# Attention loop of a decoder layer: exponentials first on ScalarE, and weight transposes and values one step earlier

## The reference

```python
xn = rms_norm(h, norm1_g)
proj = xn @ w_in                      # split into gq gk gv gr glr dq dk dv
o_gla  = gla_mixer(gq, gk, gv, gr, glr, ...)       # gated linear attention, 4 heads
o_diff = diff_attention(dq, dk, dv, ...)           # 4 heads, two score maps each
h = h + concat([o_gla, o_diff]) @ w_out
h = h + hier_moe(rms_norm(h, norm2_g), ...)        # 32 experts, top-2 of one group

# diff_attention, for each block of 128 queries
logits = q @ k.T + bias[rel_bucket(qpos - kpos)]   # causal; for comp 0 and comp 1
p = softmax(logits)
w = p[comp 0] - lam * p[comp 1]
out = rms_norm(w @ v, subln_g) * (1 - lambda_init)
```

## Time and profile before

| | us |
|---|---|
| median of 3 runs | 1276.71 (1272.01 to 1277.06) |
| the profiled execution | 1274.93 |
| its span, first to last instruction | 1273.2 |
| PE busy | 1161.4 (91%) |
| DVE busy | 873.3 (69%) |
| ACT busy | 686.3 (54%) |
| POOL busy | 229.5 (18%) |

### The profile page before, as it was taken

How to read it: one execution, slowest core, us unless ns; L and a number is a source line. 1 busy time by engine, 2 the same in 40 slices (tenths; PEclk the granted TensorE clock), 3 DMA queues, 4 the chain that set the end, 5 groups by cost and what they waited for, 6 DMA issues and landing times. The chain is left out here.

```text
span 1273.2 us, 16875 instructions
## 1 busy us (share of the span) xinstructions
PE 1161.4 (91%) x5886; PEld 874.4 (69%) x5887; DVE 873.3 (69%) x1195; ACT 686.3 (54%) x875; POOL 229.5 (18%) x265
## 2 busy tenths in 40 slices
PE   6989998889998779999539999999999999999994
PEld 5868886657665468888436777777777777777772
DVE  4434224655565566665359999999999999999882
ACT  5424204444444343432127777777777777777772
POOL 2212103221111011011022112211221222122100
PEclk9999999999999789999758999999999999999997
DMA  8120210200200244332588999999999999999941
GB/s 306 42 92 1 99 67 1 75 25 30 87 25 17 96 127 152 124 113 83 210 300 297 371 366 372 391 380 371 381 387 373 371 387 385 374 370 386 382 145 25
DMA packets 66271, 273.31 MB, mean 215 GB/s; under 512 B 12004, under 2 KB 18728, under 8 KB 41512
## 3 DMA queue, kind: packets, MB, share of 16 engines
q1 hardware_dynamic: 55592, 245.32, 50.3%
q0 software_dynamic: 7168, 20.98, 7.2%
q10 hardware_dynamic: 3456, 6.29, 1.3%
HBM read 248.44 MB, written 28.32 MB: 217 GB/s over the span
## 5 line engine op out<-in xcount | busy, mean ns | idle before, releaser
L1790 DVE TENSOR_TENSOR experts_w_low<-w_raw,experts_w_high 128x2048 fp32r<-128x2048 f32 x192 | 439.0, 2287 | 60.1 <-ACT experts_w_high L1786 60.0
L1786 ACT CAST experts_w_high<-w_raw 128x2048 fp32r<-128x2048 f32 x192 | 366.0, 1908 | 89.9 <-PE experts_py L1804 52.6
L1802 PE MATMUL experts_ph<-experts_w_high,experts_xT_high 128*96 128x512 f32 x512 | 205.1, 401 | 4.8 <-DVE experts_w_low L1790 3.6
L1803 PE MATMUL experts_ph<-experts_w_low,experts_xT_high 128*96 128x512 f32 x512 | 203.5, 397 | 0.0
L1804 PE MATMUL experts_ph<-experts_w_high,experts_xT_low 128*96 128x512 f32 x512 | 202.2, 395 | 0.0
L1718 POOL DMA_INDIRECT experts_xg<-xn_dram,experts_token x32 | 75.6, 2362 | 384.4 <-DVE experts_token L1698 384.1
L1802 PEld LDWEIGHTS experts_ph<-experts_w_high,experts_xT_high 128*96 128x96 f32 x512 | 84.7, 165 | 39.8 <-DVE experts_w_low L1790 3.7
L1804 PEld LDWEIGHTS experts_ph<-experts_w_high,experts_xT_low 128*96 128x96 f32 x512 | 83.3, 163 | 36.7
L1803 PEld LDWEIGHTS experts_ph<-experts_w_low,experts_xT_high 128*96 128x96 f32 x512 | 83.4, 163 | 33.3 <-issue 0.3
L1802 PE MATMUL experts_py<-experts_w_high,experts_hT_high 128*96 128x512 f32 x256 | 103.0, 402 | 1.2 <-DVE experts_hT_low L1921 1.2
L1803 PE MATMUL experts_py<-experts_w_low,experts_hT_high 128*96 128x512 f32 x256 | 101.8, 398 | 0.0
(11 more groups left out here) (276 smaller groups left out, 2029.3 us busy)
## 6 DMA issues: line engine op xcount, KB each, us to landing
w_raw<-in_moe_w SPq DMA_DIRECT2D x192, 1024.0 KB, 10.9
slot_raw<-in_w_in SPq DMA_DIRECT2D x12, 1024.0 KB, 7.3
front_x<-in_x SPq DMA_DIRECT2D x8, 512.0 KB, 10.9
slot_raw<-in_w_out SPq DMA_DIRECT2D x4, 1024.0 KB, 6.2
front_hx<-in_x SPq DMA_DIRECT2D x8, 512.0 KB, 4.1
out<-front_hx SPq DMA_DIRECT2D x8, 512.0 KB, 2.7
xn_dram<-front_xn SPq DMA_DIRECT2D x8, 512.0 KB, 2.8
gr_dram<-front_stage ACTq DMA_DIRECT2D x8, 256.0 KB, 2.0
```

The costliest lines, as they stand in the source:

```text
L1786: nc.scalar.copy(wh[slot(c, e)][:], raw[:, u, c, :]).then_inc(w_high, 1)
L1790: nc.vector.tensor_tensor(wl[slot(c, e)][:], raw[:, u, c, :], wh[slot(c, e)][:].bitcast(F32), ALU.subtract).then_inc(w_low, 1)
L1802: nc.tensor.matmul(out, x_hi, w_hi, start=start, stop=False)
L1803: nc.tensor.matmul(out, x_hi, w_lo, start=False, stop=False)
```

## The change

In each step of the loop, on PE the transposes of item m-1 (was m-2) and the values of item m-2 (was m-3) are issued. ACT issues the exponentials of item m first, and then the square of item m-2 and the copies of item m-1. DVE issues the norm of item m-3 ahead of `q_norm` and the maxima instead of behind them. The waits of the query tiles' transposes are set to the new items. The loop is one step shorter, and a last `norm` stands behind it on DVE.

```diff
-STEPS = N + 3
+STEPS = N + 2
@@ w_transposes
-                    for i in transposed_in.get(n + 1, []):
+                    for i in transposed_in.get(n, []):
                         pe.wait_ge(q_stored, q_number[i] + 1)
@@ PE's loop
                 if m < N:
                     scores(m)
                 fill(1)
-                if m == N + 2:
+                if m == N + 1:
                     inner(0)
-                if m >= 3:
-                    values(m - 3)
-                for g in range(groups[m - 2] if 2 <= m < N + 2 else 0):
-                    w_transposes(m - 2, g)
+                if m >= 2:
+                    values(m - 2)
+                for g in range(groups[m - 1] if 1 <= m < N + 1 else 0):
+                    w_transposes(m - 1, g)
                     fill(1)
                 for i in transposed_in.get(m, []):
-                    if m >= 2:
-                        pe.wait_ge(wT_ready, first[m - 1])
+                    if m >= 1:
+                        pe.wait_ge(wT_ready, first[m])
                     q_transposes(i)
                 fill(left)
@@ ACT's loop
             for m in range(STEPS):
-                if m >= 3:
-                    o_square(m - 3)
-                if 2 <= m < N + 2:
-                    copies(m - 2)
                 if m < N:
                     exps(m)
+                if m >= 2:
+                    o_square(m - 2)
+                if 1 <= m < N + 1:
+                    copies(m - 1)
                 for i in transposed_in.get(m, []):
                     store_transposed(i)
@@ POOL's loop
-                if m >= 3:
-                    o_root(m - 3)
+                if m >= 2:
+                    o_root(m - 2)
@@ DVE's loop
                 if 1 <= m < N + 1:
                     weights(m - 1)
+                if m >= 3:
+                    norm(m - 3)
                 for i in ended_in(m - 1):
                     if i in q_number:
                         q_norm(i)
                 if m < N:
                     maxima(m)
-                if m >= 3:
-                    norm(m - 3)
@@ behind DVE's loop
+            norm(N - 1)
             mask(0)
```

## The result

| | before | changed |
|---|---|---|
| median, us | 1276.43 (4 runs) | 1321.19 (1314.99 to 1324.86, 4 runs) |
| ratio, 95% interval | 1 | 1.0353 (1.0300 to 1.0407) |
| profiled execution / span, us | 1274.93 / 1273.2 | 1314.99 / 1313.2 |

The change makes the kernel 3.5% slower. The spans of the profiled executions differ by 40.0 us, and so does the time from the loop's first scores to the first mask behind it: 266.35 us before (195.97 to 462.32), 306.36 after (197.46 to 503.82). The profiled execution is the shortest of the changed kernel's four; by the medians the change costs 44.8 us.

What follows compares the result with a forecast made beforehand. PE's own work bounds the loop through step 27, a chain over engines the last four steps. 13.9 + 4.4 + 4.8 + 10.1 + 3.65 - 8.9 + 3.3 + 9.6 = 40.9 us on 1274.93 gives 1316 us, range 1303 to 1328.

Steps and rivals of the forecast that it cites:

- 4.4: Steps 10 and 12, after weight casts: values wait for the norm behind remainder and weights, costing 2.4 and 2.0 us.
- the drain: Last exponentials to mask: one chain of casts, remainders, norms, values 31 and square 31, 19.0 us for 15.7, +3.3.
- the ring: Steps 17 to 26: second transposes wait for scores, maxima, exponentials, square and first copy; 9.55 us a step at 768 keys.
- The first steps: Steps 1, 2, 3, 4, 6, 7: query-tile turns wait for copies behind exponentials, 13.9 us in all.
- the falls of the clock: PE's clock drops after idles over 2 us in steps 3, 6, 7, 10, 21, 23: 1.6 us each, 9.6.
- The cast steps: Steps 21 and 23, after weight casts: cast, remainder, weights, norm and maxima delay the next exponentials, 11.8 and 14.0 us.
- my ends for it: Bounds on the drain's cost: -5.4 us if values 31 did not wait for the norm, and +5 us.
- the 1.62: Idle of PE in the kernel before, at 238.86, after which the clock did not fall; used to limit clock falls.
- The rival without any new fall: PE's clock does not fall anew anywhere: 1306 us, chance 0.1.
- the rival with falls in every step: PE's clock falls in every step from 17 to 26: 1329 us, chance 0.15.
- The faster rival: Steps 28 to 31 and drain gain; earlier, second-group waits stay under PE's 4.7 us of work: 1260.6 us, chance 0.06.
- the dropped drain step: Drain after the loop: one step fewer, counted in the faster case as a gain of 5.4 us.

Runs made afterwards that it cites:

- Experiments 1 and 2: Each on the changed kernel: ACT's square and copies back ahead of exponentials, 1300.42 us; PE's projection pieces ahead of second transposes and query-tile turns, 1300.91 us.
- experiments 2 and 3: Projection pieces first on the changed kernel, 1300.91 us; on top of that, ACT's square of an ended unit ahead of the turned tile's store, 1293.27 us.
- Experiment 8: Changed kernel with the linear attention's exponents, which wait for a tile from memory, moved behind the last weights on DVE: 1316.77 us.
- experiment 7: Changed kernel with the two last weight casts on ACT one step earlier, each ahead of the square it had followed: 1310.27 us.

## Why the prediction was right, and where its terms were off

The forecast was 1316 us, with 1303 to 1328 as its range. The median is 1321.19, and the profiled execution, from which the table is taken, 1314.99.

| stretch | predicted, clock included | measured |
|---|---|---|
| steps 0 to 15 | 13.9 + 4.4 + 6.4 = +24.7 | +22.9 |
| steps 16 to 19 | +4.8 | +4.2 |
| steps 20 to 23 | 10.1 + 3.2 = +13.3 | +8.9 |
| steps 24 to 27 | +3.65 | +2.9 |
| steps 28 to exponentials 31 | -8.9 | -10.1 |
| drain to the mask | +3.3 | +11.2 |
| sum | +40.9 | +40.0 |

That the sums agree within 1 us is in part luck: five terms came out 0.6 to 4.4 us too high, 8.7 in all, and the drain 7.9 too low.

**What bounds the loop** was read rightly. PE's waits for exponentials were small because it had work, and the change put the waits onto PE. Experiments 1 and 2 cut the ring at two different points, and both bring steps 17 to 19 back to 7.6 us or less.

**The ring's length.** Predicted 8.88, 9.55 and 10.25 us for 640, 768 and 896 keys; measured 8.68 to 8.70, 9.29 and 9.38, and 9.98 to 10.08. In step 20 the second group came 6.25 us behind the scores' start for 6.4, and the next scores 3.04 behind it for 3.15. Step 27, 7.4 predicted, took 7.31.

**The first steps.** Step by step the growth was 0.5, 2.4, 3.9, 3.2, 6.1 and 1.2 us in steps 1, 2, 3, 4, 6 and 7, for 0.6, 2.3, 3.9, 3.2, 4.8 and 3.9 with the falls of the clock. The mechanism was only a part of it. The ring through the copy is there, but a second one, through the store ahead of the next square, held steps 2, 3 and 6 as well (experiments 2 and 3), and steps 4 and 6 waited above all for the norm behind the casts of steps 3 and 5 (4.46 and 2.61 us), a wait that among the first steps I had counted for 10 and 12 alone (these grew by 2.4 and 4.1 us for 4.0 and 2.0). I had said that PE would idle 2 to 6 us before the turns in steps 2 to 7; it idled 2.00, 2.67, 1.23, 0.67 and 1.99 us in steps 2, 3, 4, 6 and 7. So the sum for these steps, +22.9 for +24.7, is right partly by luck.

**The cast steps.** Steps 21 and 23 took 11.34 and 13.62 us for 11.8 and 14.0, to which I had added 1.6 each for falls of the clock. Step 21 stayed at 1.00. In step 23 the granted clock was 0.87, but the second group then waited only 0.33 us for the copy, where it waited 1.93 in step 21: the slower work of PE lay for the most part inside the ring, and adding its full price was wrong.

**The drain** is the term that was mis-sized: +3.3 predicted, +11.2 measured, outside my ends for it (-5.4 and +5). The chain was the right one. DVE and PE of the changed kernel show where it ran late: exponents waiting for their tile, norm 29, the remainder, norm 30, the mask; and values 30 and 31.

```profile
479.62 0.49 DVE L1237 TENSOR_TENSOR front_arg<-front_b_tile 128x128 f32<-128x128 f32 x2 [3.77 <-DMA front_b_tile<-b_dram]
...
483.42 0.35 DVE L1222 TENSOR_SCALAR dqT<-front_po,front_o_rs 128x128 f32<-128x128 f32 x1
...
492.47 2.35 DVE L1132 SCALAR_TENSOR_TENSOR slot_low<-slot_raw,front_out_gain,slot_high 128x2048 fp32r<-128x2048 f32 x1 [6.96 <-ACT slot_high L819]
494.74 0.34 DVE L1222 TENSOR_SCALAR dqT<-front_po,front_o_rs 128x128 f32<-128x128 f32 x1
...
503.82 0.27 DVE L1276 COPY front_sc<-front_pm 64x128 f32<-64x128 f32 x1
```

```profile
483.92 3.75 PE L618 MATMUL front_po<-dv,front_wT 128*128 128x128 f32 x16 [4.97 <-DVE dqT L1222]
...
495.23 3.65 PE L618 MATMUL front_po<-dv,front_wT 128*128 128x128 f32 x16 [4.01 <-DVE dqT L1222]
```

The tile's load waits on SP for the last spill. Before, that spill was issued 9.9 us ahead of the last exponentials' end (436.90); the shorter steps 28 to 31 left 5.3 (471.76), so the load came into the open. I had counted the steps' gain and not what had been hidden behind them. Experiment 8 prices this at 4.0 us. Each of the two values took 3.5 us, where the same work at the full clock takes 1.9 (values 29 of the kernel before, 444.62 to 446.51): the granted clock was 0.71 over the drain (0.89 before), which I had not put into this term. Before, values 30 had been slow as well (450.59 to 453.81), and values 31 not (457.34 to 459.23). By parts: the first remainder ended 17.7 us behind the last exponentials for the 11.6 predicted, with the late load and the slow values 30 ahead of it; from there to the mask were 9.0 us for 7.4, with the slow values 31 in them. The two casts in the chain, which I had counted, are 7.9 us (experiment 7).

**The clock.** I took six falls, 9.6 us, in steps 3, 6, 7, 10, 21 and 23. The granted clock fell in 3 (0.83), 6 (0.63) and 23 (0.87), and in step 12 (0.75), which I had not taken; in step 4 it was 0.76 (0.85 before). Steps 7, 10 and 21 stayed at 1.00, and two falls of the kernel before, in steps 13 (0.80) and 24 (0.83), are gone. The one in step 24 came behind an idle of 1.98 us, a row that I had not weighed against the 1.62. The rival without any new fall is refuted too. Steps 17 to 19 and 24 to 26 had idles of 1.2 to 1.7 us each, and over steps 16 to 19 and 24 to 27 the clock stayed at 1.00: the rival with falls in every step is refuted. The Trainium skill (TensorE: Matmul & The Clock Gate, "A second HAM failure mode: psum-queue depth-cycling"), weighed in the prediction, says that short idles make the clock go back and forth when they come frequently enough, and gives no size. The trace does not show it here: one such idle a step, three steps in a row, did not bring the clock down. In the first sixteen steps the mean fell to 0.90; before it was 0.97.

**The faster rival** failed where it was put: exponentials, square and copy ended at 6.2 us into step 20, PE's own work at 4.7. That the end gains was right (10.1 us), that the dropped drain step gives 5.4 was not.

## What to carry to other kernels

When two engines' orders are written by hand, an instruction moved to the front of one queue is paid for by whatever the other engine has queued behind the instruction that it pushed back: look at what stands behind each wait, and move the filler ahead of it in the same edit. Exponentials first from step 17 on are worth about 16 us here once PE's pieces stand ahead of the late transposes; in all steps and without that they cost 21 (1300.42 to 1321.19). And when a stretch gets shorter, list what was hidden behind it (a load, a cast), since that is what the next chain waits for.

## What the runs showed of the hardware that was not expected

The same idle does not always bring PE's clock down. Step 10 is written alike in the changed kernel and in the one with the exponents behind, and in both PE stood 3.25 us for the norm. In the first the piece behind it ran at the full clock of 2.4 GHz (0.24 us from matmul to matmul), and the step took 9.67 us:

```profile
285.12 0.91 PE L618 MATMUL front_po<-dv,front_wT 128*128 128x128 f32 x6 [3.25 <-DVE dqT L1222]
...
286.66 0.40 PE L534 MATMUL front_pm<-xh,slot_low 128*128 128x512 f32 x1
286.90 0.40 PE L534 MATMUL front_pm<-xh,slot_high 128*128 128x512 f32 x1
```

In the second it ran at the lower level, 1.2 GHz (0.42 us), and the step took 12.28:

```profile
287.93 1.62 PE L618 MATMUL front_po<-dv,front_wT 128*128 128x128 f32 x6 [3.25 <-DVE dqT L1222]
...
290.84 0.63 PE L534 MATMUL front_pm<-xh,slot_low 128*128 128x512 f32 x1
291.26 0.63 PE L534 MATMUL front_pm<-xh,slot_high 128*128 128x512 f32 x1
```

The changed kernel's runs spread over 9.9 us and those of the one with the exponents behind over 9.0, those of the others over 1.2 to 5.7. Only these executions were compared step by step, so whether such falls make the spread stays open.
